# 96-slot experts in five products a step, and a new order of the experts, in a mixture-of-experts pass

## The chip, the core and the metric

The kernel runs on one core of a Trainium2 chip. The time is the device time of one execution in microseconds (us). TensorE is called PE in the rows of the profile (PEld is its weight load), VectorE DVE, ScalarE ACT, GpSimd POOL and SyncE SP.

## What is computed

One step of a two-layer network on 256 tokens (128 context, 128 latent). Only the last sub-layer matters here: a mixture of eight SwiGLU experts, of which each token uses two. All of it is float32.

```python
D_MODEL = 1024; N_EXP = 8; TOP_K = 2; E_FF = 3584

def dense_swiglu(h, w_in, w_out):
    gate, up = jnp.split(h @ w_in, 2, -1)
    return (jax.nn.silu(gate) * up) @ w_out

def moe_swiglu(h, router, w_in, w_out):
    logits = (h @ router).astype(jnp.float32)
    top_val, top_idx = lax.top_k(logits, TOP_K)
    gates = jax.nn.softmax(top_val, -1)
    combine = jnp.einsum('blk,blke->ble', gates, jax.nn.one_hot(top_idx, N_EXP, dtype=jnp.float32)).astype(h.dtype)
    out = dense_swiglu(h, w_in[0], w_out[0]) * combine[..., 0:1]
    for e in range(1, N_EXP):
        out = out + dense_swiglu(h, w_in[e], w_out[e]) * combine[..., e:e + 1]
    return out
```

The 256 tokens make 512 token-expert pairs, 64 for an expert on average. With the reference's inputs the experts get, largest first, 105, 84, 76, 66, 55, 54, 39 and 33 tokens.

## The kernel before

Everything ahead of the experts (a Hyena and RWKV layer, a dense SwiGLU, a gated DeltaNet layer, the router) takes the first 1240 us and is not touched. The router's block counts the tokens of each expert and ranks the experts by their count. `perm` says which expert stands at which of the eight positions `q`, by comparing the ranks with constants of `iota` (L1818 to L1821): the even positions 0, 2, 4, 6 get the ranks 0 to 3 (the four largest experts), the odd ones the ranks 4 to 7.

`MAIN_CAPS` (L1698) gives each position its number of slots: `WIDE` is 128, `MID` is 96, `HALF` is 64. Before, it is WIDE and HALF in turns. If any expert has more tokens than its position has slots, `over` is set and all four engines run a second pass over all eight experts (`rest`, all WIDE) ahead of the main one; `more` reads that flag. Otherwise the branch skips it.

For each position the tokens' rows are gathered into slots by products with a one-hot matrix (`gather`), and then seven blocks follow (`KC` = 7; `STEPS` = 56 in all). A block reads three weight tiles of 2 MB: a gate tile and an up tile (each 1024 inputs by 512 hidden units, laid out as 8 groups of 128 rows) and an out tile (512 hidden units by 1024 outputs, 4 groups of 128 rows). In a product the slots are the stationary operand (`h[:, j, ...]`, which is loaded into the PE array, one column of the array for each slot) and the weights are the moving one:

- WIDE: for each of the 8 groups `j` one product, 128 slots by 512 weight columns (L1935). The out tile takes 4 x 2 such products (L1970).
- HALF: the array is split into two column tiles of 64 columns, named by `tile_position=(0, 0)` and `(0, 64)`. Each takes half of the weight columns, 256 at a time (L1938), and the bank then holds the halves one under the other. The out tile takes 4 x 2 products of 512 columns, one array half for each half of the output (L1973).
- MID, in the code but used by no position: twelve products a group, 32 slots by 128 weight columns each, in four column tiles of 32 (L1942 to L1947 and L1976 to L1982). The first three array quarters hold the slots 0 to 95 against the weight columns 0 to 383, the last quarter takes the columns 384 to 511 for the three slot groups in turn.

I call the work on one group, for a WIDE, MID or HALF expert, a step; a tile has 8 steps.

`pe_pass` is PE's order: gate product of block i, transposes of block i-1, up product of block i, out product of block i-1. In the first blocks of an expert it also adds the result of the expert before (`weights`, `scatter`), in the last two it gathers the tokens of the next. ACT takes the silu of the gate (L2088), copies the transposed activations (`copied`, L2050) and the finished outputs (`result`), DVE multiplies gate and up (L2132) and adds scattered results (L2106).

`sp_pass` queues the weight tiles in the order in which PE uses them, into a ring of `RING` = 7 tiles of SBUF. A tile's load is issued when PE has finished with the tile seven places before it (`s_used`). The first load of an expert can't be issued before its number is known, so all seven slots of the ring are empty of expert weights when the pass begins.

Of the kernel before, what the change touches and what calls it, by code (L numbers as in the profile page):

```python
# [11 lines left out]
ACT = mybir.ActivationFunctionType  # L12
AX = mybir.AxisListType

P = 128
# [11 lines left out]
NE = 8  # L27
# [109 lines left out]
def program(nc, A, O):  # L137
    ctx = ExitStack()
    with ctx:
# [1555 lines left out]
                norm(PAIRS - 1)  # L1695
                dve_link.sync(dve)
        WIDE, MID, HALF = T, 3 * T // 4, T // 2
        MAIN_CAPS = [WIDE, HALF] * 4  # L1698
        REST_CAPS = [WIDE] * NE

        drop(NCONST[2])
# [33 lines left out]
        with nc.Block() as block:  # L1735
# [44 lines left out]
            def _(dve):  # L1780
# [36 lines left out]

                for h in range(2):  # L1818
                    dve_link.last(dve, V.tensor_tensor(perm[:, h:NE:2, :], tokr.unsqueeze(1).broadcast_to([P, NE // 2, NE]),
                                                       cc("iota")[:, 4 * h:4 * h + 4].unsqueeze(2).broadcast_to([P, NE // 2, NE]),  # L1820
                                                       ALU.is_equal))  # L1821
                dve_link.sync(dve)
                dve_link(dve, V.tensor_tensor(tmp8, perm, rows(cc("iota")[:, 0:NE]), ALU.mult))
# [94 lines left out]
        def pe_pass(pe, m):  # L1918

            def gather(q, half):  # L1920
                c = m.caps[q]
                for j in range(4 * half, 4 * half + 4):
                    for s in range(NS):
                        mm = nc.tensor.matmul(ps[5][:, (j % 4) * T:(j % 4) * T + c], htok[:, s, j * P:(j + 1) * P], Psel[:, s, 0:c],  # L1924
                                              start=(s == 0), stop=(s == 1))
                mm.then_inc(m.gat, 1)

            def in_product(i, n, out):
                c, h = m.caps[i // KC], hA[:, (i // KC) % 2]
                m.arrived(pe, n)  # L1930
                w = m.tile(n).rearrange("p (j c) -> p j c", j=8)
                for j in range(DC):
                    start, stop = j == 0, j == DC - 1
                    if c == WIDE:
                        mm = nc.tensor.matmul(out[:], h[:, j, :], w[:, j, :], start=start, stop=stop)  # L1935
                    elif c == HALF:
                        for x in range(2):
                            mm = nc.tensor.matmul(out[HALF * x:HALF * x + HALF, 0:256], h[:, j, 0:HALF],  # L1938
                                                  w[:, j, 256 * x:256 * x + 256], start=start, stop=stop,
                                                  tile_position=(0, HALF * x))  # L1940
                    else:
                        for r in range(3):  # L1942
                            for x in range(4):
                                u, o = (x, r * P) if x < 3 else (r, 3 * P)
                                mm = nc.tensor.matmul(out[32 * x:32 * x + 32, r * P:(r + 1) * P], h[:, j, 32 * u:32 * u + 32],
                                                      w[:, j, o:o + P], start=(start and r == 0), stop=stop,
                                                      tile_position=(0, 32 * x), skip_group_check=True)  # L1947
                mm.then_inc(m.used, 1)

            def transposes(i):  # L1950
                pe.wait_ge(m.act, m.base + i + 1)
                if i:
                    pe.wait_ge(m.aT, m.base + i)
                for f in range(m.width(i) // P):
                    mm = nc.tensor.transpose(ps[4][:, f * T:(f + 1) * T], actb[:, i % 2, f * P:(f + 1) * P], ident)  # L1955
                mm.then_inc(m.tr, 1)

            def project(i):
                q, k = divmod(i, KC)
                c, n, aT = m.caps[q], out_at(i), actT[:, i % 2]  # L1960
                pe.wait_ge(m.aT, m.base + i + 1)
                if k == 0 and q:
                    pe.wait_ge(m.ye, m.base + q)
                m.arrived(pe, n)
                w = m.tile(n).rearrange("p (j c) -> p j c", j=4)
                for f in range(4):
                    start, stop = k == 0 and f == 0, k == KC - 1 and f == 3
                    for h in range(2):
                        if c == WIDE:
                            mm = nc.tensor.matmul(ps[6 + h][:], aT[:, f, :], w[:, f, 512 * h:512 * h + 512], start=start, stop=stop)  # L1970
                        elif c == HALF:
                            o = HALF * (f // 2)
                            mm = nc.tensor.matmul(ps[6][HALF * h:HALF * h + HALF, :], aT[:, f % 2, o:o + HALF],  # L1973
                                                  w[:, f, 512 * h:512 * h + 512], start=start, stop=stop, tile_position=(0, HALF * h))
                        else:
                            for r in range(3):  # L1976
                                for x in range(4):
                                    u, o = (x, r * P) if x < 3 else (r, 3 * P)
                                    a = aT[:, f, 32 * u:32 * u + 32] if f < 3 else aT[:, u, 96:128]
                                    mm = nc.tensor.matmul(ps[6 + h][32 * x:32 * x + 32, r * P:(r + 1) * P], a,  # L1980
                                                          w[:, f, 512 * h + o:512 * h + o + P], start=(start and r == 0), stop=stop,
                                                          tile_position=(0, 32 * x), skip_group_check=True)  # L1982
                mm.then_inc(m.used, 1)

            def weights(q):
                pe.wait_ge(m.Pw, m.base + q + 1)
                for s in range(NS):
                    mm = nc.tensor.transpose(ps[5][:, s * T:(s + 1) * T], Pw[:, s, :], ident)  # L1988
                mm.then_inc(m.Ct, 1)

            def scatter(q, b, bank):
                c = m.caps[q]
                for d in (2 * b, 2 * b + 1):
                    mm = nc.tensor.matmul(bank[:, (d % 2) * TT:(d % 2 + 1) * TT], ye[0:c, d * P:(d + 1) * P], Cw[0:c, :],  # L1994
                                          start=True, stop=True)
                mm.then_inc(m.sc, 1)

            pe.wait_ge(m.P, m.base + 1)
            gather(0, 0)
            pe.wait_ge(m.hA, m.base + 1)  # L2000
            gather(0, 1)
            for i in range(STEPS):
                q, k = divmod(i, KC)
                if k == 0:
                    pe.wait_ge(m.hA, m.base + 2 * q + 2)
                if i >= 2:
                    pe.wait_ge(m.act, m.base + i - 1)
                in_product(i, gate_at(i), ps[2 * (i % 2)])
                if i:
                    transposes(i - 1)  # L2010
                if k == 0 and q:
                    weights(q - 1)
                if 1 <= k <= 4 and q:
                    if k == 1:
                        pe.wait_ge(m.C, m.base + q)
                        pe.wait_ge(m.ye, m.base + q)
                    else:
                        pe.wait_ge(m.acc, m.base + 4 * (q - 1) + k - 1)
                    scatter(q - 1, k - 1, ps[5])
                if k >= 5 and q < NE - 1:  # L2020
                    if k == 5:
                        pe.wait_ge(m.P, m.base + q + 2)
                        if q:
                            pe.wait_ge(m.acc, m.base + 4 * q)
                    else:
                        pe.wait_ge(m.hA, m.base + 2 * q + 3)
                    gather(q + 1, k - 5)
                if i == STEPS - 1:
                    pe.wait_ge(m.acc, m.base + 4 * q)
                    weights(q)  # L2030
                in_product(i, up_at(i), ps[2 * (i % 2) + 1])
                if i:
                    project(i - 1)
            transposes(STEPS - 1)
            project(STEPS - 1)
            pe.wait_ge(m.act, m.base + STEPS)
            pe.wait_ge(m.aT, m.base + STEPS)
            pe.wait_ge(m.C, m.base + NE)
            pe.wait_ge(m.ye, m.base + NE)
            for b in range(4):  # L2040
                scatter(NE - 1, b, ps[BANKS[b]])

        def act_pass(act, m):

            def copied(i):
                act.wait_ge(m.tr, m.base + i + 1)
                if i >= 2:
                    m.consumed(act, out_at(i - 2))
                n = m.width(i)
                nc.scalar.activation(actT[:, i % 2].rearrange("p f t -> p (f t)")[:, 0:n], ps[4][:, 0:n], ACT.Copy).then_inc(m.aT, 1)  # L2050

            def weights(q):
                act.wait_ge(m.Ct, m.base + q + 1)
# [277 lines left out]
```

## Time and profile before

| | before |
|---|---|
| median of 3 runs | 2230.64 us (2229.3 to 2231.87) |
| profiled execution, whole | 2228.06 us |
| its span in the trace | 2226.3 us |
| the experts' products, first to last (1247.55 to 2202.5) | 955 us |
| PE busy in the span | 2032.2 us (91%) |
| mean granted clock of PE, share of full | 0.951 |

The profiled execution is 2.6 us under the median of the runs. The span leaves out 1.8 us around the traced work.

### The profile page before, as it was taken

The numbers are of one execution on the slowest core, as the hardware profiler recorded it, in microseconds if no ns is written. First come the engines' busy times: TensorE is split into PE (matmuls) and PEld (weight loads), VectorE is DVE, ScalarE is ACT, GpSimd is POOL, SyncE is SP. The second block draws the span as 40 slices with busy tenths as digits, with TensorE's granted clock in tenths as the row PEclk, the third lists the DMA queues.
The fourth block names the chain that finished last, engine by engine and source line by source line (L and its number), as shares of the span: only waits on it lengthen the run. The fifth ranks groups of instructions, "written<-read, shape, count | busy, mean of one in ns | idle before, by whom it ended". The sixth has DMA issues, their size and how long they took to land. (4 is left out here: it accounts for less than half of the span.)

```text
span 2226.3 us, 26662 instructions
## 1 busy us (share of the span) xinstructions
PE 2032.2 (91%) x11494; PEld 1420.3 (64%) x11494; DVE 609.5 (27%) x1266; ACT 314.5 (14%) x600; POOL 41.1 (2%) x65
## 2 busy tenths in 40 slices
PE   5998897888999989789887799999999999999997
PEld 3876886786888867688776444554455445544454
DVE  4436565553000046355663100000000000000002
ACT  1012222210000033222220100000000000000001
POOL 0001000000000000000000000000000000000000
PEclk9999998999999999888987899999999999999998
DMA  8729321102344152000000797999799978998794
GB/s 337 297 83 425 135 116 76 77 4 81 147 155 152 39 236 76 6 10 10 10 1 5 301 398 283 408 427 376 285 359 427 427 284 311 426 428 332 271 418 199
DMA packets 37081, 492.11 MB, mean 221 GB/s; under 512 B 4380, under 2 KB 4541, under 8 KB 7325
## 3 DMA queue, kind: packets, MB, share of 16 engines
q1 hardware_dynamic: 36956, 490.33, 54.7%
q8 instruction: 93, 1.52, 0.3%
q14 instruction: 32, 0.25, 0.0%
HBM read 487.95 MB, written 2.36 MB: 220 GB/s over the span
## 5 line engine op out<-in xcount | busy, mean ns | idle before, releaser
L1935 PE MATMUL bank<-ring,arena 128*128 128x512 f32 x896 | 395.7, 595 | 1.7 <-DMA ring<-in_experts 1.7
L1935 PEld LDWEIGHTS bank<-ring,arena 128*128 128x128 f32 x896 | 167.5, 190 | 208.8 <-issue 208.8
L1938 PE MATMUL bank<-ring,arena 128*64 128x256 f32 x1792 | 204.7, 381 | 0.0
L1970 PE MATMUL bank<-ring,arena 128*128 128x512 f32 x448 | 197.2, 593 | 0.0
L2132 DVE TENSOR_TENSOR arena<-bank,arena 128x512 f32<-128x512 f32 (+1 forms) x56 | 31.3, 558 | 597.4 <-PE bank L1935 314.1
L1938 PEld LDWEIGHTS bank<-ring,arena 128*64 128x64 f32 x1792 | 125.5, 137 | 81.1 <-issue 23.8
L1229 PE MATMUL bank<-arena,ring 128*128 128x256 f32 x704 | 155.3, 382 | 4.0 <-DVE arena L290 3.8
L1970 PEld LDWEIGHTS bank<-ring,arena 128*128 128x128 f32 x448 | 84.8, 190 | 106.8 <-issue 106.8
L1229 PEld LDWEIGHTS bank<-arena,ring 128*128 128x128 f32 x704 | 134.0, 191 | 24.5 <-issue 4.1
L2088 ACT ACTIVATE arena<-bank 128x512 f32<-128x512 f32 (+1 forms) x56 | 27.6, 492 | 787.2 <-PE bank L1935 493.5
L1350 PE MATMUL bank<-arena,ring 128*128 128x256 f32 x512 | 115.6, 388 | 6.4 <-DVE arena L290 3.8
L699 PE MATMUL bank<-arena 128*128 128x128 f32 x768 | 103.2, 291 | 14.0 <-issue 9.9
L1350 PEld LDWEIGHTS bank<-arena,ring 128*128 128x128 f32 x512 | 98.7, 194 | 24.8 <-issue 5.8
L699 PEld LDWEIGHTS bank<-arena 128*128 128x128 f32 x768 | 98.1, 205 | 19.4 <-issue 14.9
L2106 DVE TENSOR_TENSOR arena<-arena,bank 128x512 f32<-128x512 f32 x32 | 22.0, 688 | 310.6 <-PE bank L1994 310.6
L1973 PE MATMUL bank<-ring,arena 128*64 128x512 f32 x448 | 101.1, 593 | 0.5 <-ACT arena L2050 0.5
L549 PE MATMUL bank<-arena,ring 128*128 128x256 f32 (+1 forms) x416 | 92.5, 386 | 9.6 <-PEq L382 9.6
L706 PE MATMUL bank<-arena 128*128 128x128 f32 x704 | 98.2, 284 | 0.9 <-ACT arena L718 0.9
L711 PE MATMUL bank<-arena 128*128 128x128 f32 x704 | 94.4, 277 | 0.0
L549 PEld LDWEIGHTS bank<-arena,ring 128*128 128x128 f32 (+1 forms) x416 | 80.3, 193 | 21.7 <-issue 9.9
L706 PEld LDWEIGHTS bank<-arena 128*128 128x128 f32 x704 | 88.3, 197 | 2.9 <-issue 1.4
L711 PEld LDWEIGHTS bank<-arena 128*128 128x128 f32 x704 | 86.5, 194 | 0.4
(357 smaller groups left out, 2002.2 us busy)
## 6 DMA issues: line engine op xcount, KB each, us to landing
ring<-in_experts SPq DMA_DIRECT2D x168, 2048.0 KB, 13.3
ring<-in_stream SPq DMA_DIRECT2D x61, 2048.0 KB, 11.5
arena<-in_masks SPq DMA_DIRECT2D x1, 1280.0 KB, 5.9
xT<-in_xT SPq DMA_DIRECT2D x1, 1024.0 KB, 6.2
arena<-in_s0gd SPq DMA_DIRECT2D x4, 256.0 KB, 2.8
out_sgd<-arena SPq DMA_DIRECT2D x4, 256.0 KB, 2.5
out_y<-arena SPq DMA_DIRECT2D x4, 256.0 KB, 2.5
arena<-in_hfw SPq DMA_DIRECT2D x1, 544.0 KB
```

The lines of the kernel that those rows point to most:

```text
L549: mm = nc.tensor.matmul(ps[m % 4][0:rows, 0:TT], tile_in(n)[:, j, f * P:f * P + rows], hT[:, j, :], start=(j == 0), stop=(j == DC - 1))
L699: mm = nc.tensor.matmul(ps[g][:, q * T:(q + 1) * T], up[g][:, q], self.T[g][:, q], start=True, stop=True)
L706: mm = nc.tensor.matmul(ps[2 + g][:, q * T:(q + 1) * T], self.U[g][:, q], self.X[g][:, q], start=True, stop=True)
L711: mm = nc.tensor.matmul(ps[4 + g][:, q * T:(q + 1) * T], self.X[g][:, q], self.U[g][:, q], start=True, stop=True)
L1229: mm = nc.tensor.matmul(ps[4 + m % 4][:, half * TT:(half + 1) * TT], w[:, j, half * 256 + f:half * 256 + f + P], hT[:, j, :], start=(j == ...
L1350: mm = nc.tensor.matmul(ps[m % 4][:, 0:TT], tile_in(n)[:, j, f * P:(f + 1) * P], hT[:, j, :], start=(j == 0), stop=(j == DC - 1))
L1935: mm = nc.tensor.matmul(out[:], h[:, j, :], w[:, j, :], start=start, stop=stop)
L1938: mm = nc.tensor.matmul(out[HALF * x:HALF * x + HALF, 0:256], h[:, j, 0:HALF], w[:, j, 256 * x:256 * x + 256], start=start, stop=stop, til ...
L1970: mm = nc.tensor.matmul(ps[6 + h][:], aT[:, f, :], w[:, f, 512 * h:512 * h + 512], start=start, stop=stop)
L1973: mm = nc.tensor.matmul(ps[6][HALF * h:HALF * h + HALF, :], aT[:, f % 2, o:o + HALF], w[:, f, 512 * h:512 * h + 512], start=start, stop=st ...
L2088: nc.scalar.activation(sgl[:, i % 2, 0:n], ps[2 * (i % 2)][:, 0:n], ACT.Silu).then_inc(m.sil, 1)
L2132: V.tensor_tensor(actb[:, i % 2, 0:n], ps[2 * (i % 2) + 1][:, 0:n], sgl[:, i % 2, 0:n], ALU.mult).then_inc(m.act, 1)
```

## The change

`MAIN_CAPS` is now HALF, WIDE, HALF, MID, HALF, MID, HALF, MID. The comparison that makes `perm` now gives the even positions the ranks 4 to 7 and the odd ones the ranks 0 to 3. So a HALF expert comes first, the largest expert second, and the experts of the ranks 1 to 3 (84, 76 and 66 tokens) have 96 slots; the last position is one of these.

The products of a MID step are rewritten. There were twelve (which nothing used); now there are five, in column tiles of two sizes: one of 64 columns at 0 and one of 32 at 64, each against 384 weight columns, and three in the tile of 32 at 96, each against the last 128 weight columns. ACT now copies the transposed activations of a MID block in two instructions, which put the slots in order.

```diff
-        MAIN_CAPS = [WIDE, HALF] * 4
+        MAIN_CAPS = [HALF, WIDE] + [HALF, MID] * 3
...
-                                                       cc("iota")[:, 4 * h:4 * h + 4].unsqueeze(2).broadcast_to([P, NE // 2, NE]),
+                                                       cc("iota")[:, 4 - 4 * h:8 - 4 * h].unsqueeze(2).broadcast_to([P, NE // 2, NE]),
...
                     else:
+                        for lo, hi in ((0, HALF), (HALF, MID)):
+                            nc.tensor.matmul(out[lo:hi, 0:3 * P], h[:, j, lo:hi], w[:, j, 0:3 * P], start=start, stop=stop,
+                                             tile_position=(0, lo), skip_group_check=True)
                         for r in range(3):
-                            for x in range(4):
-                                u, o = (x, r * P) if x < 3 else (r, 3 * P)
-                                mm = nc.tensor.matmul(out[32 * x:32 * x + 32, r * P:(r + 1) * P], h[:, j, 32 * u:32 * u + 32],
-                                                      w[:, j, o:o + P], start=(start and r == 0), stop=stop,
-                                                      tile_position=(0, 32 * x), skip_group_check=True)
+                            mm = nc.tensor.matmul(out[MID:P, r * P:(r + 1) * P], h[:, j, 32 * r:32 * r + 32], w[:, j, 3 * P:4 * P],
+                                                  start=(start and r == 0), stop=stop, tile_position=(0, MID), skip_group_check=True)
...
-                n = m.width(i)
-                nc.scalar.activation(actT[:, i % 2].rearrange("p f t -> p (f t)")[:, 0:n], ps[4][:, 0:n], ACT.Copy).then_inc(m.aT, 1)
+                n, aT = m.width(i), actT[:, i % 2]
+                if m.caps[i // KC] == MID:
+                    blocks = ps[4][:, 0:n].rearrange("p (r t) -> p r t", r=3)
+                    nc.scalar.activation(aT[:, 0:3, 0:MID], blocks[:, :, 0:MID], ACT.Copy)
+                    nc.scalar.activation(aT[:, 3, 0:MID].rearrange("p (r t) -> p r t", r=3), blocks[:, :, MID:P], ACT.Copy)\
+                        .then_inc(m.aT, 1)
```

The out product of a MID block changes in the same way (five products for each of its 4 x 2 steps).

The order of PE's products at the start of the pass, before: the gather, then gate and up of block 0 and gate of block 1 in WIDE form.

```order
L1924 MATMUL bank<-arena 128x128 x16
L1935 MATMUL bank<-ring,arena 128x512 x24
L1955 MATMUL bank<-con,arena 128x128 x4
L1935 MATMUL bank<-ring,arena 128x512 x8
L1970 MATMUL bank<-ring,arena 128x512 x8
```

And of the changed kernel, at the same place:

```order
L1924 MATMUL bank<-arena 128x64 x16
L1938 MATMUL bank<-ring,arena 64x256 x48
L1955 MATMUL bank<-con,arena 128x128 x2
L1938 MATMUL bank<-ring,arena 64x256 x16
L1973 MATMUL bank<-ring,arena 64x512 x8
```

The first expert's products are now those of a HALF expert.

In the expert of rank 2 (position 4 before, position 5 now), PE at the end of a gate product, before:

```order
L1935 MATMUL bank<-ring,arena 128x512 x8
L1955 MATMUL bank<-con,arena 128x128 x4
L1994 MATMUL bank<-arena 128x256 x2
L1935 MATMUL bank<-ring,arena 128x512 x8
L1970 MATMUL bank<-ring,arena 128x512 x8
```

And of the changed kernel, the last two steps of the gate product and the first two of the up product:

```order
L1943 MATMUL bank<-ring,arena 64x384
L1943 MATMUL bank<-ring,arena 32x384
L1946 MATMUL bank<-ring,arena 32x128 x3
L1943 MATMUL bank<-ring,arena 64x384
L1943 MATMUL bank<-ring,arena 32x384
L1946 MATMUL bank<-ring,arena 32x128 x3
L1955 MATMUL bank<-con,arena 128x128 x3
L1996 MATMUL bank<-arena 128x256 x2
L1943 MATMUL bank<-ring,arena 64x384
L1943 MATMUL bank<-ring,arena 32x384
L1946 MATMUL bank<-ring,arena 32x128 x3
L1943 MATMUL bank<-ring,arena 64x384
```

Each step of one product of 512 columns has become five products, in which tiles of 64 and of 32 columns alternate; the transposes are three instead of four.

ACT at the end of the pass, before: the last transposed block, its copy of the result, and the squares of the final norm.

```order
L2050 ACTIVATE arena<-bank 128x256
L2056 ACTIVATE arena<-bank 128x256
L2050 ACTIVATE arena<-bank 128x256
L2066 ACTIVATE arena<-bank 64x512 x2
L258 ACTIVATE arena<-xT 128x512 x4
```

And of the changed kernel:

```order
L2064 ACTIVATE arena<-bank 128x256
L2054 ACTIVATE arena<-bank 128x3x96
L2055 ACTIVATE arena<-bank 128x96
L2077 ACTIVATE arena<-bank 96x384
L2079 ACTIVATE arena<-bank 32x128 x3
L2077 ACTIVATE arena<-bank 96x384
L2079 ACTIVATE arena<-bank 32x128 x3
L258 ACTIVATE arena<-xT 128x512 x4
```

Three copies there have become ten.

## Rows read from the trace of the kernel before

**Rows 1.** The page: busy time of the engines, and 40 slices of the span.

```profile
PE 2032.2 (91%) x11494; PEld 1420.3 (64%) x11494; DVE 609.5 (27%) x1266; ACT 314.5 (14%) x600; POOL 41.1 (2%) x65
...
PE   5998897888999989789887799999999999999997
...
DMA  8729321102344152000000797999799978998794
```

**Rows 2.** The page: lines of the chain that ended last, shares of the span.

```profile
PE bank L1935 17%; PE bank L1938 9%; PE bank L1970 9%; PE bank L1973 4%; PE bank L1994 1%; PE bank L1924 1%; PE bank L1955 1%; DMA ring<-in_experts 0%; PE bank L264 0%; DVE arena L277 0%; DVE arena L284 0%; DVE rstd L273 0%; PE bank L1988 0%; ACT arena L2066 0%; DVE xT L2202 0%
```

**Rows 3.** Busy time by stretch, one expert each: WIDE, HALF, WIDE, HALF.

```profile
core 0: us, PE busy (x) PEld busy (x) DVE busy (x) ACT busy (x) POOL busy (x), PEclk, DMA share, GB/s
1247.55:1391.26 143.71, 143.71 (x376) 66.61 (x377) 5.75 (x11) 8.07 (x16) 0.00 (x0) 1.00 0.90 361
1391.26:1478.69 87.43, 87.43 (x627) 49.34 (x627) 6.62 (x15) 8.01 (x19) 0.00 (x0) 1.00 0.99 414
1478.69:1631.66 152.97, 152.97 (x414) 70.77 (x412) 8.49 (x15) 9.62 (x19) 0.00 (x0) 1.00 0.86 340
1631.66:1719.20 87.54, 87.54 (x628) 49.45 (x628) 6.62 (x15) 8.01 (x19) 0.00 (x0) 1.00 0.99 414
```

**Rows 4.** PE in order of time, a WIDE block: start, us, line, tile, count.

```profile
1268.22 0.60 PE L1955 MATMUL bank<-con,arena 128*128 128x128 f32 x4
1268.66 7.03 PE L1935 MATMUL bank<-ring,arena 128*128 128x512 f32 x16
1275.53 7.03 PE L1970 MATMUL bank<-ring,arena 128*128 128x512 f32 x16
1282.40 7.03 PE L1935 MATMUL bank<-ring,arena 128*128 128x512 f32 x16
1289.26 0.60 PE L1955 MATMUL bank<-con,arena 128*128 128x128 f32 x4
```

**Rows 5.** PE in order of time, a HALF block.

```profile
2147.61 3.60 PE L1973 MATMUL bank<-ring,arena 128*64 128x512 f32 x16
2151.04 3.62 PE L1938 MATMUL bank<-ring,arena 128*64 128x256 f32 x32
2154.60 0.44 PE L1955 MATMUL bank<-con,arena 128*128 128x128 f32 x2
2154.87 1.03 PE L1994 MATMUL bank<-arena 128*128 128x256 f32 x4
2155.83 3.67 PE L1938 MATMUL bank<-ring,arena 128*64 128x256 f32 x32
2159.34 3.60 PE L1973 MATMUL bank<-ring,arena 128*64 128x512 f32 x16
```

**Rows 6.** PE in order of time, early: products in four column tiles (L345).

```profile
45.77 3.70 PE L345 MATMUL bank<-ring,silc 128*32 128x128 f32 x128 [1.12 <-DVE mod L364]
```

**Rows 7.** The instructions of L345: count, duration in ns (min/median/max), first and last start.

```profile
L345 PEld LDWEIGHTS bank<-ring,silc x1536: 106/110/177, 40.0 to 428.8; 128*32 128x32 f32 x192
L345 PE MATMUL bank<-ring,silc x1536: 269/273/422, 40.0 to 428.9; 128*32 128x128 f32 x192
```

**Rows 8.** Busy time by short stretch, where a HALF product begins.

```profile
1391.25:1391.30 0.05, 0.05 (x3) 0.04 (x2) 0.00 (x0) 0.00 (x0) 0.00 (x0) 1.00 0.01 0
1391.30:1391.50 0.20, 0.20 (x3) 0.16 (x4) 0.00 (x0) 0.00 (x0) 0.00 (x0) 1.00 0.20 82
```

**Rows 9.** PE in order of time, last WIDE product and first HALF one.

```profile
1390.74 0.59 PE L1970 MATMUL bank<-ring,arena 128*128 128x512 f32 x1
1391.26 1.30 PE L1938 MATMUL bank<-ring,arena 128*64 128x256 f32 x10
```

**Rows 10.** Weight stream: rate in one stretch, and PE's only wait for it.

```profile
1680.00:1700.00 20.00, 20.00 (x152) 11.72 (x150) 1.62 (x4) 1.98 (x5) 0.00 (x0) 1.00 1.01 427
...
PE bank L1935 <- DMA ring<-in_experts: 1.7, 1, 1.7
```

**Rows 11.** Groups by line and shape, 1247 to 2203: busy us, mean ns.

```profile
L2050 ACT ACTIVATE arena<-bank 128x512 f32<-128x512 f32 x28 | 16.6, 593 | 0.8 <-PE bank L1955 0.8
...
L2050 ACT ACTIVATE arena<-bank 128x256 f32<-128x256 f32 x28 | 10.8, 385 | 7.0 <-PE bank L1955 7.0
...
L2066 ACT ACTIVATE arena<-bank 64x512 f32<-64x512 f32 x8 | 4.8, 594 | 33.1 <-PE bank L1973 33.0
```

**Rows 12.** All engines in order of time, end of the pass.

```profile
2197.01 0.39 ACT L2050 ACTIVATE arena<-bank 128x256 f32<-128x256 f32 x1 [6.96 <-PE bank L1955]
...
2201.15 1.20 ACT L2066 ACTIVATE arena<-bank 64x512 f32<-64x512 f32 x2 [3.75 <-PE bank L1973]
...
2202.49 4.54 PE L1994 MATMUL bank<-arena 64*128 64x256 f32 x16 [1.39 <-ACT arena L2066]
```

More of the change, by code:

```diff
@@ L1975, in project @@
                         else:
+                            o = 512 * h
+                            for lo, hi in ((0, HALF), (HALF, MID)):
+                                nc.tensor.matmul(ps[6 + h][lo:hi, 0:3 * P], aT[:, f, lo:hi], w[:, f, o:o + 3 * P], start=start, stop=stop,
+                                                 tile_position=(0, lo), skip_group_check=True)
                             for r in range(3):
[L1977 to L1982, printed above, removed]
+                                mm = nc.tensor.matmul(ps[6 + h][MID:P, r * P:(r + 1) * P], aT[:, f, 32 * r:32 * r + 32],
+                                                      w[:, f, o + 3 * P:o + 4 * P],
+                                                      start=(start and r == 0), stop=stop, tile_position=(0, MID),
+                                                      skip_group_check=True)
                 mm.then_inc(m.used, 1)
@@ L2048, in copied @@
                     m.consumed(act, out_at(i - 2))
-                n = m.width(i)
-                nc.scalar.activation(actT[:, i % 2].rearrange("p f t -> p (f t)")[:, 0:n], ps[4][:, 0:n], ACT.Copy).then_inc(m.aT, 1)
+                n, aT = m.width(i), actT[:, i % 2]
[4 more added lines that the diff above has]
+                        .then_inc(m.aT, 1)
+                else:
+                    nc.scalar.activation(aT.rearrange("p f t -> p (f t)")[:, 0:n], ps[4][:, 0:n], ACT.Copy).then_inc(m.aT, 1)
             def weights(q):
```

## Prediction

> **What bounds the kernel now.** I read the page first: the 40 slices show PE at nine tenths or more from the experts' start on, while DMA moves between 7 and 9 [rows 1], and the chain that ended last is made of the experts' products, L1935, L1938, L1970 and L1973, 39% of the span [rows 2]. Then the stretches, one for each expert: in each of them PE is busy for all of it, at the full clock of 2.4 GHz (PEclk 1.00), and a WIDE expert takes 152.97 us, a HALF one 87.5 us [rows 3]. The weight stream runs at 427 GB/s where nothing holds it [rows 10], so a tile of 2.097 MB takes 4.91 us and an expert's 21 tiles 103.1 us. The stream is the slower of the two in a HALF expert and waits for the ring in a WIDE one (0.86 against 0.99 DMA share); the ring of 7 tiles, 34 us of stream, carries PE over the difference of 15.6 us. PE waits for a weight tile once, for 1.7 us [rows 10]. So PE bounds the experts, by 955 us against 168 x 4.91 = 825 us of stream. Only 130 us lie between them, and a faster PE can't win more.
>
> **One WIDE block, one HALF block.** A WIDE tile takes 6.87 us (1268.66 to 1275.53) and four transposes 0.44, so a block is 3 x 6.87 + 0.44 = 21.05 us [rows 4]. Each product stands in the rows as two records (16 for 8 products); I call each a pass. In a HALF tile two column tiles work at once: 16 records of 512 columns take 3.43 us (2147.61 to 2151.04) [rows 5], so 0.429 us for two records, which is the price of one record of 512 columns in the WIDE form (6.87 / 16). A pass of 384 columns is then 0.322 us. Four column tiles of 32 work at once too: 128 records of 128 columns take 3.70 us from the first start to the last end [rows 6]; less the last one's own length, 0.27 [rows 7], that is 27 ns a record and 0.108 us for a pass of each of the four.
>
> **Part 1, MID in place of WIDE, three experts.** A MID step has three tiles of the array with equal work: tile A (64 columns) two passes of 384, 0.644 us; tile B (32) the same; tile C (32) three products, six passes of 0.108, 0.648 us. If the tiles run side by side a step takes 0.65 us and a weight tile 8 x 0.65 = 5.20 us. Changing between 128-column transposes and split products costs something: the HALF block spends 3.43, 3.56 and 3.51 us on its three products instead of three times 3.43, 0.21 us more [rows 5], and 0.09 more is my allowance at the transposes; with three transposes (0.33) a MID block is 15.60 + 0.21 + 0.09 + 0.33 = 16.23 us. Against 21.05 that is -4.82 us, and there are 21 such blocks: **-101 us**. A MID and a HALF expert together then take PE 152.97 - 33.7 + 87.5 = 206.8 us, and the stream 42 x 4.91 = 206.2 us: the two are level. The largest expert ahead of them fills the ring, so each HALF expert starts with seven tiles in hand, uses up some three and a half, and gets them back in the next MID one. I take no stall there.
>
> Whether the tiles do run side by side when their sizes differ is what decides this case, and no row shows it: every split stage before uses one size. What the rows show is this. At the start of a HALF product three records run in the first 50 ns, one of them the end of the product before, so both tiles start together and none follows in the next 200 ns [rows 8]. In the four-tile stage each tile keeps its own pace. If records had to start in the order of the program, with both passes of a product behind each other, each of four products would hold up the next by a pass, and a round would take 8 x 0.108 / 2 = 0.43 us where 0.216 is measured [rows 6]. So products queue by tile. A change of size, where the new tile lies on columns that the old one uses, costs: the first HALF record starts 0.52 us after the last WIDE one, 0.09 us more than the 0.43 of its columns [rows 9]. With columns of their own, as A, B and C have, nothing in the trace says that they wait, and nothing says that they don't. I take side by side, as the nearest rows (two tiles, four tiles) have it, by a small margin.
>
> The Trainium skill has a rule against this (TensorEngine Tiling, Key Properties): a change of tiling mode, and not merely of tile, drains TensorE, and it lists 128 x 64 and 128 x 32 as two modes. The trace agrees as far as it goes (the 0.09 us at [rows 9]), and it is the first rival below. The skill also says (TensorE: Matmul & The Clock Gate, what overlaps and what doesn't) that matmuls start and end strictly in program order; with a product's passes behind each other, the four-tile stage here speaks against it, 0.216 us a round and not 0.43.
>
> **Part 2, a HALF expert first.** The ring holds no expert weights at the start: tile 0 is there at 1247.5 us and the others follow each 4.91 us. PE would be done with a first HALF expert quickly: 87.43 us is the second expert's stretch [rows 3], of which 7.06 are the last out product of the WIDE one before it and some 4.3 the scatter of its result (four times 0.96) and the weights' transposes, so 76.0. The first product of the second expert needs tile 20, which lands at 1247.5 + 20 x 4.91 = 1345.7; PE is ready at 1323.5. **+22 us** of waiting, spread over that expert. Before, a WIDE expert hid this whole start. Between two products PE then waits some 1.4 us at a time; I price the clock at full, since the rows that follow have 1.00.
>
> **Part 3, ACT.** Its copies lie beside PE's tiles of 3.4 us and more, but not at the end. By 593 ns for 512 and 385 ns for 256 elements [rows 11], an ACT copy takes about 178 ns and 0.81 ns for each element: 0.41 and 0.26 us for the two transposed copies in place of 0.39 (**+0.3**), and 2 x 0.49 + 6 x 0.28 = 2.7 us for the eight copies of the result in place of 1.20, for which PE waits [rows 12] (**+1.5**). In the middle of the pass `result` of a MID expert has to be done while PE runs the next gate product (3.5 us): 2.7 us and a wait's end fit, just; a miss would cost below 1 us, three times at most. The DVE comparison that makes `perm` has the same size: nothing. Gathers for 96 slots cost what those for 128 and 64 do, to 0.2 us.
>
> **The sum.** -101 + 22 + 2 = **-77 us** from 2228.06, the profiled execution: 2151 us. The runs' median is 2.6 us above it, so **2153 us**, 3.5% faster. Bounds of this case alone: a MID tile of 5.16 (the bare columns) to 5.45 us gives -103 to -85, the start 15 to 25 us, so 2136 to 2172.
>
> **Rivals.**
> 1. *Tiles of different sizes don't run side by side (slower).* A has the array for itself, then B and C together, and each change of size costs the 0.09 us of [rows 9], twice a step: 0.644 + 0.09 + 0.648 + 0.09 = 1.47 us a step, 11.8 a tile, 36.0 a MID block, 15.0 more than WIDE. 21 x 15.0 = +315, and +24 of the other parts: 2567, as a median **2570 us**, up to 2590 with a late weight load behind each change. PE then bounds everything and the stream idles. For it: each change of size in the trace costs something, whatever the sizes. Against it: those changes are on shared columns. By the skill's rule above it comes out here.
> 2. *They run side by side only in part.* Where records have to start in program order the step is 0.322 + 0.322 + 5 x 0.108 = 1.18 us (A's second pass, B's second, then C's six): a tile 9.5, +8.0 a block, +168 + 24: **2423 us**. If C's weight loads, of 110 ns [rows 7], were not hidden, six times 0.218 = 1.31 us would give 2490. Against both stands the four-tile stage [rows 6].
> 3. *No difference.* The step would have to be about 0.80 us, between the WIDE form's 0.86 and 0.65: from there on the change loses. I know no mechanism for just that.
> 4. *The slots don't suffice*, the flag is set and the second pass runs: eight WIDE experts, 8 x 153 = 1224 us on top, **3450 us**. The counts 105, 84, 76, 66 and 55, 54, 39, 33 leave 12 slots at 96 and 9 at 64.
>
> **Chances.** My forecast 0.52, rival 1 0.36, rival 2 0.09, no difference 0.02, the flag 0.01. Within 0.2% is about what a measurement of this kernel can't tell from no change. Faster 0.52, same 0.02, slower 0.46. The likeliest case's own range is 2136 to 2172; to leave out no more than two tenths the range has to reach rival 1: 2136 to 2590.
>
> **What would show it.** In PE's order of time a MID tile of 5.2 us and a step of 0.65 confirm part 1; 11.8 us and weight loads that begin only when the tile before has ended are rival 1; 9.5 is rival 2. PE should wait for `in_experts` about 22 us in all, before 1350 us, and not later; if waits come in the MID experts too, the stream is slower than 427 GB/s or the ring runs empty. The wait ahead of the last L1996 should be 2.9 us instead of 1.39. I am wrong at once if the tiles of different sizes exclude each other; all else moves the time by 20 us at most.

## The result, and the profile after

| | before | after |
|---|---|---|
| median | 2230.64 us (2229.3 to 2231.87) | 2609.44 us (2608.46 to 2610.68) |
| ratio | | 1.170, 95% interval 1.167 to 1.173 |
| profiled execution, its span | 2228.06, 2226.3 us | 2608.46, 2606.7 us |
| PE busy in the span | 2032.2 us (91%) | 2393.2 us (92%) |

The changed kernel is 17% slower, 379 us. My forecast was 2153 us. The time is nearest to that of my first rival, in which tiles of different sizes don't run side by side (2570, up to 2590), and even that was 19 us short.

The page of the changed kernel, busy time and three rows of the 40 slices, as in [rows 1]:

```profile
PE 2393.2 (92%) x15505; PEld 1624.1 (62%) x15505; DVE 605.8 (23%) x1266; ACT 316.2 (12%) x639; POOL 41.2 (2%) x65
...
PE   5988878899998988887789999999999999999997
...
PEclk8998988999999988987899999999999999999998
DMA  7556311033415100000999799444697444994410
```

PE is at nine tenths as before, its clock too, but DMA falls to 4 in three long stretches where it was 7 to 9. Something on PE holds the weights back there. The stretches, one for each expert (HALF, WIDE, HALF, MID, HALF, MID), stand against [rows 3]:

```profile
core 0: us, PE busy (x) PEld busy (x) DVE busy (x) ACT busy (x) POOL busy (x), PEclk, DMA share, GB/s
1250.02:1348.44 98.42, 81.04 (x588) 47.18 (x589) 3.87 (x11) 6.99 (x16) 0.00 (x0) 0.98 1.01 428
1348.44:1501.20 152.76, 152.76 (x412) 70.75 (x412) 8.50 (x15) 9.62 (x19) 0.00 (x0) 1.00 0.88 351
1501.20:1588.66 87.46, 87.46 (x628) 49.47 (x627) 6.62 (x15) 7.80 (x19) 0.00 (x0) 1.00 0.98 412
1588.66:1853.93 265.27, 265.27 (x1687) 133.19 (x1685) 7.55 (x15) 8.98 (x25) 0.00 (x0) 1.00 0.52 198
1853.93:1946.62 92.69, 92.69 (x693) 52.65 (x691) 6.62 (x15) 9.28 (x26) 0.00 (x0) 1.00 0.94 392
1946.62:2211.90 265.28, 265.28 (x1687) 133.19 (x1685) 7.55 (x15) 8.98 (x25) 0.00 (x0) 1.00 0.52 196
```

PE counts as busy for all of a MID expert, 265.27 of 265.27 us, so the busy share doesn't show what is lost; only the length of the stretch does. A MID expert takes 265.27 us, a WIDE one 152.76: 112.5 us more, where 33.7 less were forecast. The HALF expert behind a MID one takes 92.69 instead of 87.46, since the MID expert's last out product stands in it. Both three times make 3 x (112.5 + 5.2) = 353 us. The first HALF expert takes 98.4 us instead of the 76.0 worked out for it, +22.4. With 1.8 us for ACT at the end, and 2.5 us by which the experts began later (1250.02 and not 1247.55; in the six kernels below they begin between 1246.3 and 1250.4, so this may well be chance), that is 379.7 of the 380.4 us between the spans.

One MID step, PE and its weight loads in order of time (start, us, engine, line, tile, count; in brackets the idle time before):

```profile
1591.74 0.19 PEld L1943 LDWEIGHTS bank<-ring,arena 128*64 128x64 f32 x2 [0.20 <-issue]
1591.74 1.30 PE L1943 MATMUL bank<-ring,arena 128*64 128x384 f32 x3
1592.53 0.11 PEld L1943 LDWEIGHTS bank<-ring,arena 128*32 128x32 f32 x1 [0.60 <-issue]
1592.54 0.11 PEld L1946 LDWEIGHTS bank<-ring,arena 128*32 128x32 f32 x1
1592.54 0.52 PE L1946 MATMUL bank<-ring,arena 128*32 128x128 f32 x3
...
1592.88 0.49 PE L1943 MATMUL bank<-ring,arena 128*32 128x384 f32 x1
1592.89 0.49 PE L1946 MATMUL bank<-ring,arena 128*32 128x128 f32 x3
1593.31 0.19 PEld L1943 LDWEIGHTS bank<-ring,arena 128*64 128x64 f32 x2 [0.20 <-issue]
```

The 64-column product starts at 1591.74 with its two passes. The first weights for a 32-column tile are loaded at 1592.53, after 0.60 us in which nothing was loaded, and the products of both small tiles start together at 1592.54. The next 64-column product begins at 1593.31. So A has 0.80 us alone, B and C have 0.77 us together, and the step takes 1.57 us.

### The profile page after: what moved, and what is told of

Same layout as the page of the kernel before. It is cut to its first block, busy times and chain, and to the rows that moved or that the text cites. A ratio compares the mean times of both kernels' runs of the same rounds, so it can differ in the third digit from the quotient of the medians.

```text
span 2606.7 us, 34723 instructions
## 1 busy us (share of the span) xinstructions
PE 2393.2 (92%) x15505; PEld 1624.1 (62%) x15505; DVE 605.8 (23%) x1266; ACT 316.2 (12%) x639; POOL 41.2 (2%) x65
## 4 chain that ended last, share of the span: by engine, by line
PE 48%; DMA 4%; DVE 0%; issue 0%; SPq 0%; ACT 0%; DVEq 0%
PE bank L1943 15%; PE bank L1978 7%; PE bank L1938 6%; PE bank L1946 6%; PE bank L1935 4%; DMA ring<-in_experts 4%; PE bank L1973 3%; PE bank L1981 3%; PE bank L1970 2%; PE bank L1996 1%; PE bank L1955 1%; PE bank L1924 1%; PE bank L264 0%; SPq L1902 0%; DVE arena L277 0%
## 5 line engine op out<-in xcount | busy, mean ns | idle before, releaser
L1943 PE MATMUL bank<-ring,arena 128*64 128x384 f32 (+1 forms) x1344 | 528.9, 505 | 0.0
L1946 PE MATMUL bank<-ring,arena 128*32 128x128 f32 x2016 | 283.1, 277 | 0.0
L1943 PEld LDWEIGHTS bank<-ring,arena 128*64 128x64 f32 (+1 forms) x1344 | 110.8, 121 | 270.8 <-issue 270.6
L1978 PE MATMUL bank<-ring,arena 128*64 128x384 f32 (+1 forms) x672 | 264.5, 505 | 0.6 <-ACT arena L2055 0.6
L2140 DVE TENSOR_TENSOR arena<-bank,arena 128x256 f32<-128x256 f32 (+2 forms) x56 | 28.5, 508 | 808.7 <-PE bank L1946 345.4
L1946 PEld LDWEIGHTS bank<-ring,arena 128*32 128x32 f32 x2016 | 192.9, 109 | 0.0
L2096 ACT ACTIVATE arena<-bank 128x256 f32<-128x256 f32 (+2 forms) x56 | 25.3, 452 | 1106.9 <-PE bank L1946 660.4
L1981 PE MATMUL bank<-ring,arena 128*32 128x128 f32 x1008 | 141.6, 277 | 0.0
L1978 PEld LDWEIGHTS bank<-ring,arena 128*64 128x64 f32 (+1 forms) x672 | 55.3, 121 | 134.4 <-issue 133.2
L699 PE MATMUL bank<-arena 128*128 128x128 f32 x768 | 102.7, 290 | 14.0 <-issue 9.9
L699 PEld LDWEIGHTS bank<-arena 128*128 128x128 f32 x768 | 97.6, 204 | 19.4 <-issue 14.9
L706 PE MATMUL bank<-arena 128*128 128x128 f32 x704 | 99.1, 286 | 1.6 <-ACT arena L718 1.6
L1935 PE MATMUL bank<-ring,arena 128*128 128x512 f32 x224 | 99.1, 595 | 1.2 <-DMA ring<-in_experts 1.2
```

The source lines that it names most:

```text
L699: mm = nc.tensor.matmul(ps[g][:, q * T:(q + 1) * T], up[g][:, q], self.T[g][:, q], start=True, stop=True)
L706: mm = nc.tensor.matmul(ps[2 + g][:, q * T:(q + 1) * T], self.U[g][:, q], self.X[g][:, q], start=True, stop=True)
L1943: nc.tensor.matmul(out[lo:hi, 0:3 * P], h[:, j, lo:hi], w[:, j, 0:3 * P], start=start, stop=stop, tile_position=(0, lo), skip_group_check= ...
L1946: mm = nc.tensor.matmul(out[MID:P, r * P:(r + 1) * P], h[:, j, 32 * r:32 * r + 32], w[:, j, 3 * P:4 * P], start=(start and r == 0), stop=s ...
L1978: nc.tensor.matmul(ps[6 + h][lo:hi, 0:3 * P], aT[:, f, lo:hi], w[:, f, o:o + 3 * P], start=start, stop=stop, tile_position=(0, lo), skip_g ...
L1981: mm = nc.tensor.matmul(ps[6 + h][MID:P, r * P:(r + 1) * P], aT[:, f, 32 * r:32 * r + 32], w[:, f, o + 3 * P:o + 4 * P], start=(start and ...
```

## Experiments

Two groups of runs, each timed in three rounds beside the kernel before. The names: "order only", "six products", "five sorted", "twelve products", "six, 128 slots first" and "five, 128 slots first". All compute the whole step. The median of the kernel before was 2229.74 us beside the first four and 2231.12 us beside the last two.

| kernel | median us | ratio to before (95%) |
|---|---|---|
| order only | 2252.38 | 1.010 (1.009 to 1.012) |
| six products | 2157.99 | 0.967 (0.966 to 0.969) |
| five sorted | 2490.72 | 1.117 (1.115 to 1.119) |
| twelve products | 2305.75 | 1.034 (1.032 to 1.036) |
| six, 128 slots first | 2137.94 | 0.958 (0.957 to 0.960) |
| five, 128 slots first | 2583.87 | 1.158 (1.156 to 1.160) |

### The order alone

```diff
-        MAIN_CAPS = [HALF, WIDE] + [HALF, MID] * 3
+        MAIN_CAPS = [HALF, WIDE] * 4
```

> The new order of the experts alone (a 64-slot expert first), all large experts with 128 slots in one product a step. Both theories: only the wait for the weight stream in the first expert is added, 22 us (tile 20 lands at 1247.5 + 20 x 4.91 = 1345.7 us, TensorE would be ready at 1323.5). 2230.6 + 22 = 2253 us, 2248 to 2258. If it is above 2265, the order costs more than that wait, and less of the changed kernel's 379 us belongs to its five products.

Measured 2252.38 us, 22.6 above the kernel before in the same group (2229.74). In the trace the waits for the stream stand in the HALF form only, and once ahead of the WIDE expert:

```profile
PE bank L1938 <- DMA ring<-in_experts: 9.1, 9, 1.2
PE bank L1973 <- DMA ring<-in_experts: 6.8, 6, 2.2
...
PE bank L1935 <- DMA ring<-in_experts: 1.2, 1, 1.2
```

(total us, times, longest.) They add up to 17 us and not to 22. Each of the 16 is counted from the modelled end of a record, some 0.17 us after the time at which the next one would have started, which is 2.7 us more, and the granted clock of this expert was 0.97, up to 2.6 us more. So the order costs what the first expert lacks in weights, and nothing else that shows.

### One size for all tiles

```diff
-                        for lo, hi in ((0, HALF), (HALF, MID)):
+                        for lo, hi in ((0, 32), (32, 64), (64, 96)):
```

The same in the out product: A's work in two tiles of 32 columns.

> The changed kernel with the 64-column product of each step split into two 32-column products (tiles at 0, 32, 64 and 96, all of one size, six products a step). Theory A (tiles of different sizes exclude each other): side by side again, 0.65 us a step, 5.2 us a tile, 2153 us, 2140 to 2175. Theory B (what is slow is the last tile with its three short products and six weight loads, whatever the sizes): the step stays near 1.5 us and the time near 2600 us. Theory C (products are held to program order, two records each): 1.18 us a step or more, about 2420 us.

Measured 2157.99 us. Theory A gave 2153; B and C are out by 260 us and more. The step, PE in order of time:

```profile
1592.13 0.50 PE L1943 MATMUL bank<-ring,arena 128*32 128x384 f32 x3
1592.20 0.49 PE L1946 MATMUL bank<-ring,arena 128*32 128x128 f32 x3
1592.45 0.50 PE L1943 MATMUL bank<-ring,arena 128*32 128x384 f32 x3
1592.53 0.49 PE L1946 MATMUL bank<-ring,arena 128*32 128x128 f32 x3
```

Three 384-column passes start together every 0.32 us (1592.13, 1592.45), with three passes of the last tile beside them: two of these make a step of 0.65 us. And by expert, the first MID one and the HALF one after it:

```profile
1588.56:1709.34 120.78, 120.78 (x2009) 113.93 (x2007) 7.56 (x15) 9.18 (x25) 0.00 (x0) 1.00 1.00 423
1709.34:1796.13 86.79, 86.23 (x717) 52.07 (x720) 6.63 (x15) 9.26 (x26) 0.00 (x0) 1.00 1.00 423
```

120.8 us for the MID expert (forecast 119.3), 207.6 for the two (forecast 206.8), with the stream at its full share all the time. There is one more product a step than in the changed kernel (two more records and two more weight loads), and it runs 451 us faster. The split of the 64-column product is the only edit, so what is slow there is the mixture of sizes.

### The same five products, sorted by size

```diff
+                for j in range(DC if c == MID else 0):
+                    nc.tensor.matmul(out[0:HALF, 0:3 * P], h[:, j, 0:HALF], w[:, j, 0:3 * P], start=(j == 0), stop=(j == DC - 1),
+                                     tile_position=(0, 0), skip_group_check=True)
                 for j in range(DC):
...
-                        for lo, hi in ((0, HALF), (HALF, MID)):
+                        for lo, hi in ((HALF, MID),):
```

> The changed kernel's five products, but sorted: for each weight tile first all eight 64-column products, then all 32-column ones. So the size changes twice a tile and not sixteen times. If tiles of different sizes exclude each other AND each change costs the measured extra (1.57 us a step less 0.644 and 0.648 = 0.28 us for two changes): 8 x 0.644 + 8 x 0.648 + 0.28 = 10.6 us a tile, 15.3 less than 12.55 x 21 x 3 suggests... in numbers: 63 tiles x 1.95 us = 123 us off 2609, 2486 us. If only the changes cost and different sizes can run side by side otherwise: about 5.5 us a tile, 2175 us.

The out product is sorted in the same way. Measured 2490.72 us, 119 us less than the changed kernel; both effects at work gave 2486, changes alone 2175. One tile, PE in order of time:

```profile
1585.33 5.32 PE L1933 MATMUL bank<-ring,arena 128*64 128x384 f32 x16
1590.59 0.51 PE L1946 MATMUL bank<-ring,arena 128*32 128x384 f32 x1
1590.59 0.52 PE L1949 MATMUL bank<-ring,arena 128*32 128x128 f32 x3
...
1595.95 0.44 PE L1958 MATMUL bank<-con,arena 128*128 128x128 f32 x2
```

The 64-column products take 5.26 us and the small ones 5.36 after them, 10.62 a tile. So the loss of a MID tile in the changed kernel against 5.2 us has two parts: 5.4 us that stay in the sorted form, because one size stands still while the other works (0.3 of it the two changes that are left), and 12.55 - 10.62 = 1.9 us for fourteen more changes of size, 0.14 us each. The first is about three quarters. By itself the sorted form doesn't show that the sizes exclude each other: its small products stand behind eight 64-column ones, and PE may not reach so far ahead. In the changed kernel they stand right behind one, and wait all the same.

### Twelve products, one size

```diff
-                        for lo, hi in ((0, HALF), (HALF, MID)):
-                            nc.tensor.matmul(out[lo:hi, 0:3 * P], h[:, j, lo:hi], w[:, j, 0:3 * P], start=start, stop=stop,
-                                             tile_position=(0, lo), skip_group_check=True)
                         for r in range(3):
+                            for x in range(3):
+                                nc.tensor.matmul(out[32 * x:32 * x + 32, r * P:(r + 1) * P], h[:, j, 32 * x:32 * x + 32],
+                                                 w[:, j, r * P:(r + 1) * P], start=(start and r == 0), stop=stop,
+                                                 tile_position=(0, 32 * x), skip_group_check=True)
```

> The changed kernel with twelve products of 32 slots by 128 weight columns a step, all tiles of one size (the form that stood unused before, with the new order and slots). Theory A: the same columns for each tile as with six products, 0.65 us a step, 2153 us, 2140 to 2180. If the rate of instructions matters (48 records of weight loads and products in 0.65 us, 13.5 ns each, through a whole expert and not in bursts as in the early four-tile stage), it is slower than the six products by a share that grows with the length of the expert; from 2200 us up would show that.

The out product changes in the same way. Measured 2305.75 us, 148 above the six products, though each tile of the array streams the same columns. In between, the products do keep their pace, and then everything on PE stops:

```profile
1601.08 0.27 PE L1947 MATMUL bank<-ring,arena 128*32 128x128 f32 x1
1601.09 0.28 PE L1944 MATMUL bank<-ring,arena 128*32 128x128 f32 x2
1603.88 0.27 PE L1944 MATMUL bank<-ring,arena 128*32 128x128 f32 x1 [2.51 <-issue]
1603.89 0.30 PE L1947 MATMUL bank<-ring,arena 128*32 128x128 f32 x1
```

The wait ends on no semaphore ("issue"), and it stands in the middle of a tile, between two groups that need nothing new. The waits of this kind, by line, in the expert stage (PE; total us, times, longest):

```profile
PE bank L1944 <- issue: 59.5, 33, 2.8
...
PE bank L1947 <- issue: 18.0, 10, 2.8
PE bank L1980 <- issue: 16.3, 11, 2.7
...
PE bank L1983 <- issue: 4.5, 2, 2.8
```

98 us in 56 stops, where the six products have none; two more stops in other lines add 4 us. Most of the rest of the 148 us is the clock. The three MID experts (the first of them below) have a mean granted clock of 0.93 or 0.94, where it was 1.00 with six products. In the second row, right behind a stop that ended at 1701.57, it is 0.50, the lower level of 1.2 GHz:

```profile
1589.69:1761.39 171.70, 137.29 (x3928) 124.35 (x3927) 7.56 (x15) 9.13 (x25) 0.00 (x0) 0.93 0.79 308
1702.30:1705.60 3.30, 3.30 (x72) 3.28 (x64) 1.07 (x3) 0.00 (x0) 0.00 (x0) 0.50 0.65 154
```

That makes up to 34 us over the three. Another 9 us is the 0.16 us at each stop by which the modelled end of a record lies behind the next start.

This is the second branch of what I expected, a limit on the rate of instructions. The page has instruction packets of 16 KB: 132 with six products, 179 with twelve.

```profile
q8 instruction: 179, 2.93, 0.5%
```

The 47 packets more are for 12096 records and weight loads more (48835 instructions in the trace and 36739), 257 a packet. The stops keep to the same count. Between the ends and starts of neighbouring stops, two stretches:

```profile
1597.67:1601.37 3.70, 3.70 (x128) 3.49 (x128) 0.00 (x0) 0.00 (x0) 0.00 (x0) 1.00 1.02 430
1603.88:1616.11 12.23, 12.23 (x254) 8.48 (x254) 1.25 (x4) 2.21 (x5) 0.00 (x0) 1.00 1.01 426
```

128 products' records and 128 weight loads, or about twice that. All other stretches between two stops come to about a multiple of 128 too. And each of the 55 stops of more than 0.3 us ends 2.2 to 3.0 us after the start of a 16 KB instruction packet; the one shown above, which ends at 1603.88, after the packet of 1601.29. So it is likely that PE runs out of instructions and waits for the next packet. It isn't shown, since no run changed the supply alone.

### The old order, with six and with five products

```diff
-        MAIN_CAPS = [HALF, WIDE] + [HALF, MID] * 3
+        MAIN_CAPS = [WIDE, HALF] + [MID, HALF] * 3
...
-                                                       cc("iota")[:, 4 - 4 * h:8 - 4 * h].unsqueeze(2).broadcast_to([P, NE // 2, NE]),
+                                                       cc("iota")[:, 4 * h:4 * h + 4].unsqueeze(2).broadcast_to([P, NE // 2, NE]),
```

The run with six products has the three tiles of 32 columns from above as well.

> Six products of one size a step, and the old order: the 128-slot expert first, a 64-slot one last. If the first expert's wait for the stream (22 us) is the whole price of the new order and the smaller experts need no more of the ring, this takes it back, and 2 us of the last copies too: 2158 - 24 = 2134 us, 2128 to 2142. If the stream (825 us for all weights, 206.2 for a 96-slot and a 64-slot expert together against 206.8 of TensorE) becomes the bound instead, the waits come back in later experts, and it stays at 2150 us or more.

> The changed kernel's five products with the old order of the experts. The step stays 1.57 us, so only the first expert's wait goes: 2609 - 24 = 2585 us, 2578 to 2592. If order and form worked on each other (for instance the clock fell in the first expert and came back late), it would be outside of that.

Six products: 2137.94 us, 20.1 less than with the new order (expected 24). Against the kernel before (2231.12 in that group) it is 4.2% faster, the fastest version here. The stream is nearly the bound now; in its trace a few waits come back in the later experts:

```profile
PE bank L1973 <- DMA ring<-in_experts: 4.0, 4, 1.5
PE bank L1938 <- DMA ring<-in_experts: 3.0, 3, 1.2
...
PE bank L1943 <- DMA ring<-in_experts: 1.2, 1, 1.2
```

8 us in all, 5.4 of them in the last expert; with the new order there were 3.4 us of such waits behind the first expert. The 5 us of difference are about what the gain lacks to 24. A MID and a HALF expert together need as long on PE (206.5 us) as on the stream (206.2), so that little is left in hand fits this. Five products: 2583.87 us, 25.6 less than the changed kernel, expected 24. So the order is worth 20 to 26 us in all three forms (22.6 with 128 slots in every large expert), and order and form hardly work on each other.

## Why the prediction was wrong

**What bounds the kernel before.** Right: order only and six products moved as the division of PE and stream says, within 1 and 5 us.

**Part 1, the step.** This is the step that failed, at the sentence "I take side by side, as the nearest rows (two tiles, four tiles) have it, by a small margin". Those rows show tiles of equal size, and the six products confirm them for a whole expert (0.65 us a step, 120.8 us an expert, against 0.65 and 119.3). They say nothing of unequal ones. With a 64-column tile beside 32-column ones on other columns, the trace shows A alone and then B and C, 1.57 us. The prediction said itself that "nothing in the trace says that they wait, and nothing says that they don't", and then chose by the nearest rows, against what was there: the change of size had an unhidden start, [rows 9]. I read its 0.09 us as the price of sharing columns. The changed kernel and the sorted five products show that a change costs no less (0.14 us) where no column is shared, so sharing isn't needed for it. By the Trainium skill's rule (TensorEngine Tiling, Key Properties), which I had cited, the tiles come out one after the other here; the trace agrees, with weight loads for one size that start only when the columns of the other have gone through (0.60 us of idle weight loading at 1592.53).

**The size of rival 1.** It was 1.47 us a step by [rows 9] and is 1.57: A takes 0.80 instead of 0.74, and B and C 0.77 instead of 0.74. Each change has the gap of 0.09 us, and besides the second pass behind it starts late: A's at 1592.12, 0.37 us after the first, of which 0.32 are its columns, and the small ones' by 0.03 us. Why is not shown. The sum's term was 339 us, of which 315 for the step; measured it is 353 for the step.

**Part 2, the order.** Right: +22 us forecast, +22.4 in the stretches, +22.6 as a time. The clock, which I had priced at full, stood at 0.98 in the first expert and at 1.00 after it.

**Part 3, ACT.** Right. The wait ahead of the last product is 2.90 us as forecast:

```profile
2580.71 0.49 ACT L2077 ACTIVATE arena<-bank 96x384 f32<-96x384 f32 x1 [12.74 <-PE bank L1981]
2581.21 0.84 ACT L2079 ACTIVATE arena<-bank 32x128 f32<-32x128 f32 x3
...
2583.54 3.69 PE L1996 MATMUL bank<-arena 96*128 96x256 f32 x16 [2.90 <-ACT arena L2079]
```

**The level pair.** The forecast that a MID and a HALF expert need as much of the stream as of PE holds. That no wait follows holds in the changed kernel only because its PE is so slow; with six products there were 3.4 us of such waits with the new order (2158 us against 2153), and 8 us with the old one.

**Rivals 2 to 4.** Rival 2 (program order) is out by the six products, 0.65 us a step where it asks for 1.18 or more. Rival 3 (no difference) is out by the time. The flag wasn't set: no second pass stands in any trace.

**The range.** Its lower end, 2136, doesn't follow from the terms given for it: -103, +15 and +2 on 2231 make 2145. This has no part in the miss.

## What to carry to other kernels

Column tiles of TensorE ran side by side here only while all of them had one size (64 with 64, 32 with 32; 64 beside 32 did not, and no other pair was run): split the largest piece down to the size of the smallest (six equal products, 3 to 4% faster) rather than save a product by a wide one (five unequal products, 17% slower). Where a rule speaks against a change and the trace has no row of the disputed case, the nearest rows on both sides don't decide it; a single kernel with one size would have. And the first stage after an empty ring wants the work that takes longest per byte: the 128-slot expert first was worth 20 to 26 us.

## What the runs showed of the hardware

- Products in column tiles of 64 and of 32 exclude each other even on columns of their own: 0.80 us for the one, 0.77 for the others, in turn. Sorted by size, 5.26 and 5.36 us a tile.
- A change between these sizes costs 0.14 us (1.9 us for fourteen of them): a gap of 0.09 us, and a second pass that starts 0.03 to 0.05 us late.
- Twelve products of 128 columns a step keep the array's pace between stops, 3.7 us at the shortest, but not for a whole expert: PE stood still 56 times, up to 2.8 us, 98 us in all, with about 256 records and weight loads or a multiple between two stops, and the granted clock fell to 0.93 or 0.94 on average. With six products a step (24 records and weight loads in 0.65 us instead of 48) there was no such stop, and the clock was 1.00.
